# A two-block transformer kernel: end of a gate product, memory scores, squares and latent keys put in other places

## Chip, core and metric

The kernel runs as one program on one core of a Trainium2 chip. The metric is the device time of one execution in microseconds (us); less is better. TensorE (PE) multiplies, VectorE (DVE), ScalarE (ACT) and GpSimd (POOL) do elementwise work, SyncE (SP) issues most transfers. Each engine runs its own instructions strictly in order and waits on semaphores for the others.

## What is computed

Two transformer blocks over 512 rows of 1024 features, in float32. The first block mixes a short convolution, latent attention (MLA, 8 heads) and retention (4 heads) with 16 meta tokens ahead; the second sums three gated branches (gated linear attention, GLA; sparse attention, DSA; attention to a memory, MEM) and ends in 16 experts. What matters here:

```
y = concatenate([y_conv, y_mla, y_ret]);  x = x + y @ w_out        # first block
h = rmsnorm(x, g_mix)                                              # "h2" in the kernel
...
k = rmsnorm(mem_h @ w_kv keys);  o_mem = softmax(q k^T) v          # 4 heads of 256
gate = sigmoid(h @ w_gates + b)
merged = gate0*(o_gla @ w_o_gla) + gate1*(o_dsa @ w_o_dsa) + gate2*(o_mem @ w_o_mem)
x = x + merged @ w_out_2;  x = x + experts(rmsnorm(x))
```

## The kernel before

Every weight product is kept at nearly full float32 precision with three matmuls for one: weights and activations are split into a rounded part (`w_hi`, `act_hi`) and the rest (`w_lo`, `act_lo`). Weights arrive in units of 128 x 1024 into four slots of `raw`. For each unit ScalarE writes `w_hi` by a copy with rounding (`split_high`), then GpSimd subtracts it for `w_lo` (`split_low`). A product such as `gate10` is four units (u0 to u3), each met by four blocks of 128 rows (b0 to b3; memory products have b0 and b1). A `part` is one unit with one block: 2 chunks x 3 matmuls of 128 x 128 x 512, and one accumulating PSUM bank per block. `split_upto` places the split of the unit two ahead at the part with b0.

One list, `make_order()`, is walked by all engines; each has a function for a step or skips it. So the list sets the order of every engine. `spread(these, those)` puts the steps of `those` evenly between the steps of `these`: the parts of products fill TensorE's time while heads go through scores, softmax and values.

- MLA: `mla_transposes(h)` turns queries and keys of head h into `qT` and `kT` (h % 2 picks the buffer). ScalarE copied `qT` from PSUM bank 6 and VectorE copied `kT` (96 x 528) from banks 4 and 5 (`k_transposed`). Between the two heads of a pair stand parts of `ret_qk`; VectorE rotates each finished block of it (`rope_turn`, six operations).
- Norm of h2: `norm_scale("h2")` is four squares on ScalarE with row sums (`Square`, 128 x 1024), a reciprocal root in small steps shared by ScalarE (Ln, Exp) and VectorE, then four scalings on VectorE into `xs`. `norm("h2")` turns them on TensorE. `mem_scale("k")` is the same root for the memory keys `mk`, after `mem_kv0` and `mem_kv1`.
- DSA: 32 pairs j (8 heads x 4 blocks of rows). Step j has `dsa_scores(j)`, one or two parts, `dsa_values(j-2)` and `dsa_turn(j-1)`, which waits for the scaled probabilities of VectorE. `mix_dsa(h)` splits a head's output for the product `w_o10` into `mix_hi` (ScalarE) and `mix_lo` (VectorE). When all of `w_o01` is done, the waiting ones go out together.
- MEM: 16 pairs in the same pattern, with parts of `gate20` between.

When the last block of a gate product is accumulated, ScalarE loads the sigmoid table, waits for VectorE's four `gate_sum`, does a sigmoid of 128 x 2048 and loads the old table back.

Of the kernel before, what the change touches and what calls it, by code (L numbers as in the profile page):

```python
# [17 lines left out]
ACTF = mybir.ActivationFunctionType  # L18
# [227 lines left out]
def make_order():  # L246
# [4 lines left out]
    order += [("mla_norm", t) for t in range(2, NT + 1)] + item("mla_z")  # L251
    order += mla_order() + item("mem_kv0") + [("barrier", "gla"), ("norm_scale", "h2")] + item("mem_kv1") + [("mem_scale", "k")]
    order += item("mem_kv2") + [("norm", "h2"), ("mem_prepare", "k")] + item("mem_kv3")
# [59 lines left out]
def program(nc, w, out, known):  # L313
# [12 lines left out]
    with ExitStack() as ctx:  # L326
# [625 lines left out]
        def _(pe):  # L952
# [118 lines left out]

            def attention_transposes(tag, h, width, q_bank, k_bank, q_src, k_src):
# [6 lines left out]
                claim(k_bank, (DVE, ("kT", tag, h)))  # L1079
                claim(k_bank + 1, (DVE, ("kT", tag, h)))  # L1080
                pe.transpose(ps[0:width, k_bank, SEQ - N_META:SEQ], k_src(NT)[0:N_META, :], ident[0:N_META, 0:N_META])
                for t in range(NT):
                    tr = pe.transpose(ps[0:width, k_bank + 1, P * t:P * t + P], k_src(t), ident[:, :])
                tr.then_inc(*PE.done(("kT", tag, h)))

            def mla_scores(j):
                _, t, h, i = turn_of(j)
                n = P * (t + 1)
                if t == 0:
                    pe.wait_ge(*ACT.after("qT", "mla", h))  # L1090
                    pe.wait_ge(*DVE.after("kT", "mla", h))
# [38 lines left out]
            def mla_transposes(h):  # L1130
                if h == 0:
                    pe.wait_ge(*DVE.after("rope_m", "q", NT - 1, 5))
                    pe.wait_ge(*DVE.after("rope_m", "k", NT, 5))
                attention_transposes("mla", h, QKH, 6, 4, lambda t: q_sb[:, t, QKH * h:QKH * (h + 1)],
                                     lambda t: k_sb[:, t, QKH * h:QKH * (h + 1)])

            def ret_transposes(p):
                if p == 0:
                    pe.wait_ge(*DVE.after("rope_r", NT - 1, 5))
                    pe.wait_ge(*DVE.after("rope_r", NT, 5))  # L1140
                attention_transposes("ret", p, P, 0, 1, lambda t: rqk[:, t, P * p:P * (p + 1)],
                                     lambda t: rqk[:, t, 256 + P * p:256 + P * (p + 1)])

# [504 lines left out]
        def _(act):  # L1648
# [21 lines left out]
            def rsqrt_start(key, v):  # L1670
# [5 lines left out]
                nc.scalar.activation(v[1], v[1], ACTF.Exp, scale=-0.5).then_inc(*ACT.done(("y0", *key)))  # L1676

            def norm_scale(name):

# [3 lines left out]
                if name == "mem":  # L1683
# [5 lines left out]
                    act.wait_ge(mem_landed, 32)  # L1689
                act.wait_ge(*DVE.after("ss0", name))  # L1690
                for i, (src, scaled, rows) in enumerate(tiles):
                    for key in NORM_NEEDS(name, i):
                        act.wait_ge(*key[0].after(*key[1]))
                    nc.scalar.activation(scaled, src, ACTF.Square,
                                         accum_out=ss[0:rows, 0, i:i + 1]).then_inc(*ACT.done(("ss", name, i)))
                n = len(tiles)
# [416 lines left out]
            def q_transposed(tag, h, width, dst, bank):  # L2113
# [80 lines left out]
            for step, *a in order:  # L2194
# [18 lines left out]
                elif step == "norm_scale":  # L2213
                    norm_scale(*a)
                elif step == "conv":
                    for b in range(2):
# [17 lines left out]
        def _(dve):  # L2234
# [14 lines left out]
            def norm_scale(name):  # L2249

                tiles = NORM_TILES[name]
                n = len(tiles)
                if name != "h":
                    dve.memset(ss[:, 0:3, 0:n], 1.0).then_inc(*DVE.done(("ss0", name)))
# [610 lines left out]

            def k_transposed(tag, h, width, dst, bank):
                dve.wait_ge(*PE.after("kT", tag, h))
                if h >= 2:
                    dve.wait_ge(*PE.after(*last_scores(h - 2)))
                dve.tensor_copy(dst[0:width, h % 2, :],  # L2870
                                psf[0:width, (bank + 1) * SEQ - N_META:(bank + 2) * SEQ]).then_inc(*DVE.done(("kT", tag, h)))

            def mla_scores(j):
# [91 lines left out]
            for step, *a in order:  # L2965
                if step == "constants":
                    dve.memset(ss[:, 0:3, 0:NT + 1], 1.0).then_inc(*DVE.done(("ss0", "h")))
# [3 lines left out]
                elif step == "part":  # L2971
                    if a[0] in META_COLS and a[2] == "meta":
                        meta_add(*a[0:2])
                    elif a[1] == n_units(a[0]) - 1:
                        evict(a[0], a[2])
                elif step == "mla_transposes":
                    k_transposed("mla", a[0], QKH, kT, 4)
                elif step == "dsa_turn":
# [86 lines left out]
```

## Time and profile before

| | |
|---|---|
| three runs | 1498.11 us median (1496.21 to 1498.94) |
| profiled execution | 1493.74 us, its span on the core 1491.9 us |
| mean granted TensorE clock | 0.957 |
| TensorE busy | 1358.6 us, 91% of the span |
| VectorE, ScalarE, GpSimd busy | 600.3, 533.5, 417.3 us |

The span is what the views below cover; 1.84 us of the profiled time lie around it. In a row of the timeline the first number is the start in us from the span's start, the second the duration, then engine, line of the source, operation, what it writes and reads, the count, and in brackets the idle time before it with the work that ended it. Where rows are merged (x4) the second number is the whole stretch.

### The profile page before, as it was taken

How to read it: one execution, taken by the hardware profiler on the slowest of the kernel's cores; microseconds unless marked ns; L12 is line 12 of the kernel's file. 1: busy time of each engine (PE TensorE's matmuls, PEld its weight loads, DVE VectorE, ACT ScalarE, POOL GpSimd, SP SyncE). 2: the span in 40 equal slices, each digit the busy share in tenths (PEclk: the TensorE clock that was granted, in tenths of full speed). 3: DMA queues.
4: the chain of work that ended last, by engine and by line, in shares of the span. 5: the costliest groups of instructions: out<-in, count | busy, mean ns of one | idle time of the engine just before them, and what ended most of it. 6: DMA issues, size and time to landing. Idle time of an engine off the chain costs nothing.

```text
span 1491.9 us, 16432 instructions
## 1 busy us (share of the span) xinstructions
PE 1358.6 (91%) x6192; PEld 1003.2 (67%) x6192; DVE 600.3 (40%) x1340; ACT 533.5 (36%) x947; POOL 417.3 (28%) x202
## 2 busy tenths in 40 slices
PE   4999889888989999999998899899899997799996
PEld 3778666556767776675776787688787786444443
DVE  2086644444350114435897444214333315222125
ACT  4352322334463446444433545223534323101111
POOL 3155311001555341322433222344105331000002
PEclk9999898998999999999999999999999997799999
DMA  4132432303335130221322111243016524889925
GB/s 141 57 106 57 127 113 79 95 29 99 121 109 183 57 113 15 85 71 52 90 92 78 43 57 64 89 145 98 8 65 203 191 77 170 355 309 375 333 79 185
DMA packets 76440, 179.62 MB, mean 120 GB/s; under 512 B 11182, under 2 KB 22756, under 8 KB 69700
## 3 DMA queue, kind: packets, MB, share of 16 engines
q1 hardware_dynamic: 68656, 165.48, 33.0%
q0 software_dynamic: 2592, 8.41, 1.5%
q10 hardware_dynamic: 5108, 4.62, 1.1%
q8 instruction: 52, 0.85, 0.2%
q14 instruction: 32, 0.26, 0.1%
HBM read 153.32 MB, written 25.17 MB: 120 GB/s over the span
## 4 chain that ended last, share of the span: by engine, by line
PE 42%; DVE 9%; ACT 2%; issue 1%; DMA 1%; POOL 0%; DVEq 0%; ACTq 0%
PE ps L963 8%; PE ps L1445 8%; PE ps L965 7%; PE ps L964 7%; PE ps L1452 4%; DVE work L2512 1%; PE ps L1322 1%; DVE dq L2521 1%; DVE best L2510 1%; PE ps L1339 1%; PE ps L1438 1%; PE ps L1295 1%; PE ps L1367 1%; DVE mix_lo L2285 1%; PE ps L1329 1%
## 5 line engine op out<-in xcount | busy, mean ns | idle before, releaser
L847 POOL TENSOR_TENSOR w_lo<-raw,w_hi 128x1024 fp32r<-128x1024 f32 (+1 forms) x158 | 379.0, 2415 | 817.5 <-ACT w_hi L1659 817.5
L963 PE MATMUL ps<-w_hi,act_hi 128*128 128x512 f32 (+1 forms) x560 | 236.7, 423 | 6.5 <-POOL w_lo L847 3.6
L1659 ACT ACTIVATE w_hi<-raw 128x1024 fp32r<-128x1024 f32 (+1 forms) x158 | 158.7, 1032 | 182.2 <-PE ps L965 175.0
L964 PE MATMUL ps<-w_lo,act_hi 128*128 128x512 f32 (+1 forms) x560 | 221.6, 396 | 0.0
L965 PE MATMUL ps<-w_hi,act_lo 128*128 128x512 f32 (+1 forms) x560 | 220.8, 394 | 0.0
L963 PE MATMUL ps<-w_hi,mix_hi 128*128 128x512 f32 x320 | 132.8, 415 | 15.3 <-DVE mix_lo L2285 11.8
L963 PEld LDWEIGHTS ps<-w_hi,act_hi 128*128 128x128 f32 (+1 forms) x560 | 106.0, 189 | 46.6 <-issue 14.4
L965 PE MATMUL ps<-w_hi,mix_lo 128*128 128x512 f32 x320 | 128.0, 400 | 0.0
L964 PE MATMUL ps<-w_lo,mix_hi 128*128 128x512 f32 x320 | 127.9, 400 | 0.0
L965 PEld LDWEIGHTS ps<-w_hi,act_lo 128*128 128x128 f32 (+1 forms) x560 | 105.5, 188 | 25.6
L964 PEld LDWEIGHTS ps<-w_lo,act_hi 128*128 128x128 f32 (+1 forms) x560 | 105.9, 189 | 24.8 <-issue 2.5
L1445 PE MATMUL ps<-gu,xeT 128*128 128x512 f32 x256 | 117.5, 614 | 1.6 <-DVE xeT L2734 1.6
L963 PE MATMUL ps<-act_hi,w_hi 128*128 128x512 f32 (+4 forms) x280 | 105.5, 379 | 8.9 <-POOL w_lo L847 8.4
L964 PE MATMUL ps<-act_lo,w_hi 128*128 128x512 f32 (+4 forms) x280 | 105.6, 379 | 0.0
L965 PE MATMUL ps<-act_hi,w_lo 128*128 128x512 f32 (+4 forms) x280 | 104.4, 376 | 0.0
L1445 PEld LDWEIGHTS ps<-gu,xeT 128*128 128x128 f32 x256 | 49.2, 197 | 58.8 <-issue 58.8
L963 PEld LDWEIGHTS ps<-w_hi,mix_hi 128*128 128x128 f32 x320 | 62.1, 194 | 31.1 <-DVE mix_lo L2285 12.9
L964 PEld LDWEIGHTS ps<-w_lo,mix_hi 128*128 128x128 f32 x320 | 62.1, 194 | 13.6 <-issue 0.7
L965 PEld LDWEIGHTS ps<-w_hi,mix_lo 128*128 128x128 f32 x320 | 62.0, 194 | 13.5
L963 PEld LDWEIGHTS ps<-act_hi,w_hi 128*128 128x128 f32 (+2 forms) x280 | 52.3, 187 | 21.9 <-issue 5.6
L924 POOL DMA_INDIRECT yg<-y_rows,pos_main x8 | 8.4, 1054 | 194.2 <-DMA y_rows<-ye 192.1
L965 PEld LDWEIGHTS ps<-act_hi,w_lo 128*128 128x128 f32 (+2 forms) x280 | 52.5, 188 | 12.0 <-issue 1.3
(451 smaller groups left out, 1994.0 us busy)
## 6 DMA issues: line engine op xcount, KB each, us to landing
raw<-in_w_in SPq DMA_DIRECT2D x92, 512.0 KB, 3.6
gu<-in_w_gate SPq DMA_DIRECT2D x16, 1024.0 KB, 6.3
gu<-in_w_up SPq DMA_DIRECT2D x16, 1024.0 KB, 8.4
dn<-in_w_down SPq DMA_DIRECT2D x16, 1024.0 KB, 9.7
x_rows<-zeros SPq DMA_DIRECT2D x16, 512.0 KB, 4.9
raw<-in_w_out SPq DMA_DIRECT2D x16, 512.0 KB, 3.9
raw<-in_w_mem_kv SPq DMA_DIRECT2D x16, 512.0 KB, 3.6
xe<-x_rows SPq DMA_DIRECT2D x16, 512.0 KB, 9.1
```

What stands on the lines that cost most here:

```text
L847: pool.tensor_tensor(lo[:, 0:a], raw[:, g % RAW_SLOTS, 0:a], hi[:, 0:a].bitcast(F32), ALU.subtract).then_inc(*POOL.done(("w_lo", g)))
L963: pe.matmul(dst, l_hi, r_hi, start=start, stop=False, skip_group_check=skip)
L964: pe.matmul(dst, l_hi, r_lo, start=False, stop=False, skip_group_check=skip)
L965: return pe.matmul(dst, l_lo, r_hi, start=False, stop=stop, skip_group_check=skip)
L1295: pe.matmul(ps[:, bank, 0:n], iqT[rows, h // 2, P * t:P * t + P], ikT[rows, 0:n], start=True, stop=True).then_inc(*PE.done(("rel", t, h)))
L1322: pe.matmul(ps[:, 4 + j % 2, 0:n], dqT[:, h, P * t:P * t + P], dkT[:, h // DSA_G, 0:n], start=True, stop=True).then_inc(*PE.done(("d_S", j)))
L1329: tr = pe.transpose(ps[:, 6, P * b:P * b + P], d_prob[:, j % 3, P * b:P * b + P], ident[:, :])
L1339: mm = pe.matmul(ps[:, 7, P * t:P * t + P], dv[:, b, P * g:P * g + P], d_probT[:, j % 2, P * b:P * b + P], start=(b == 0), stop=(b == t))
L1367: mm = pe.matmul(ps[:, 4 + j % 2, 0:MEM], mqT[:, 2 * h + c, P * t:P * t + P], mkT[:, 2 * h + c, :], start=(c == 0), stop=(c == 1))
L1445: mm = pe.matmul(ps[:, bank, :], xeT[:, i, k, :], gu[s][:, :, k, :], start=(k == 0), stop=(k == KC - 1))
L1452: mm = pe.matmul(ps[:, 5 + n, :], hidT[:, i, P * c:P * c + P], dn[s][:, c, 512 * n:512 * n + 512], start=(c == 0), stop=(c == 1))
L1659: nc.scalar.activation(split_slot(g)[0][:, 0:a], raw[:, g % RAW_SLOTS, 0:a], ACTF.Copy).then_inc(*ACT.done(("w_hi", g)))
```

## The change

Four places of the order, and one move between engines:

1. Of the 48 parts of `gate01`, `w_o01` and `gate10` between the sparse pairs, the last four (`gate10` u3, b0 to b3) now stand behind the last `mix_dsa`, just ahead of `w_o10`. The other 44 are spread over the 35 steps, so 9 steps have two parts where 13 had.
2. At the first memory scores a part of `gate20` stands after pair 0 and one after pair 1; one stood there after pair 1 alone.
3. The four squares of the norm of h2 stand between the parts of `mem_kv1`, one ahead of each pair of parts; what follows of `norm_scale` stands behind `mem_kv1`.
4. The copies of the latent keys `kT` go from VectorE to ScalarE, behind those of `qT`.

```diff
-    order += mla_order() + item("mem_kv0") + [("barrier", "gla"), ("norm_scale", "h2")] + item("mem_kv1") + [("mem_scale", "k")]
+    order += mla_order() + item("mem_kv0") + [("barrier", "gla"), ("norm_square", "h2", 0)]
+    order += [x for i in range(1, NT) for x in item("mem_kv1")[2 * i - 2:2 * i] + [("norm_square", "h2", i)]]
+    order += item("mem_kv1")[6:] + [("norm_scale", "h2"), ("mem_scale", "k")]
...
-    for step in [x for s in spread(steps, [[p] for p in item("gate01", "w_o01", "gate10")]) for x in s]:
+    dense = item("gate01", "w_o01", "gate10")
+    for step in [x for s in spread(steps, [[p] for p in dense[:-4]]) for x in s]:
...
-    order += done + item("w_o10", "gate11", "w_o11", "mem_q0") + [("mem_scale", "q0")]
+    order += done + dense[-4:] + item("w_o10", "gate11", "w_o11", "mem_q0") + [("mem_scale", "q0")]
...
-    order += [x for s in spread(steps, [[p] for p in g2 if p[3] < 3]) for x in s] + [p for p in g2 if p[3] == 3]
+    free = [p for p in g2 if p[3] < 3]
+    order += steps[0] + free[0:1] + steps[1] + free[1:2]
+    order += [x for s in spread(steps[2:], [[p] for p in free[2:]]) for x in s] + [p for p in g2 if p[3] == 3]
...
+            def norm_square(name, i):
+
+                if i == 0:
+                    act.wait_ge(*DVE.after("ss0", name))
+                src, scaled, rows = NORM_TILES[name][i]
...
+                nc.scalar.activation(scaled, src, ACTF.Square,
+                                     accum_out=ss[0:rows, 0, i:i + 1]).then_inc(*ACT.done(("ss", name, i)))
...
+            def k_transposed(tag, h, width, dst, bank):
+                act.wait_ge(*PE.after("kT", tag, h))
+                nc.scalar.activation(dst[0:width, h % 2, :], psf[0:width, (bank + 1) * SEQ - N_META:(bank + 2) * SEQ],
+                                     ACTF.Copy).then_inc(*ACT.done(("kT", tag, h)))
...
                 elif step == "mla_transposes":
                     q_transposed("mla", a[0], QKH, qT, 6)
+                    k_transposed("mla", a[0], QKH, kT, 4)
```

ScalarE from the end of `mem_kv0` (`xs` is a square's output, `w_hi` a unit's split, `ss` 128x4 the root for h2 and 128x8 that for the memory keys, `m_sq` and `mk` the squares and copy of a finished memory block, `mv_new` a block of `mem_kv2`). Before:

```order
L1694 ACTIVATE xs,ss<-x_56 128x1024 x4
L1674 ACTIVATE ss<-ss 128x4
L1676 ACTIVATE ss<-ss 128x4
L1659 ACTIVATE w_hi<-raw 128x1024 x4
L1838 ACTIVATE m_sq<-ps 128x512
L1840 ACTIVATE mk<-ps 128x512
L1838 ACTIVATE m_sq<-ps 128x512
L1840 ACTIVATE mk<-ps 128x512
L1674 ACTIVATE ss<-ss 128x8
L1676 ACTIVATE ss<-ss 128x8
L1659 ACTIVATE w_hi<-raw 128x1024 x4
L1840 ACTIVATE mv_new<-ps 128x512 x2
```

Now, from the third split of this stretch; three squares with two splits between them stand ahead of it:

```order
L1664 ACTIVATE w_hi<-raw 128x1024
L1690 ACTIVATE xs,ss<-x_56 128x1024
L1664 ACTIVATE w_hi<-raw 128x1024
L1850 ACTIVATE m_sq<-ps 128x512
L1852 ACTIVATE mk<-ps 128x512
L1850 ACTIVATE m_sq<-ps 128x512
L1852 ACTIVATE mk<-ps 128x512
L1679 ACTIVATE ss<-ss 128x4
L1681 ACTIVATE ss<-ss 128x4
L1679 ACTIVATE ss<-ss 128x8
L1681 ACTIVATE ss<-ss 128x8
L1664 ACTIVATE w_hi<-raw 128x1024 x4
```

The four splits that stood behind all squares now stand one behind each square, and both roots have moved together, right ahead of the next four splits.

VectorE at the same place, from the last step of the root for h2 (`xs` are the four scalings, the reduction of `m_sq` a memory block's sum). Before:

```order
L2246 SCALAR_TENSOR_TENSOR ss<-ss 128x4
L2260 TENSOR_SCALAR xs<-x_56,ss 128x1024 x4
L2392 TENSOR_REDUCE ss<-m_sq 128x2 x2
L2237 TENSOR_SCALAR ss<-ss 128x8
L2242 SCALAR_TENSOR_TENSOR ss<-ss 128x8
L2244 TENSOR_TENSOR ss<-ss 128x8
L2246 SCALAR_TENSOR_TENSOR ss<-ss 128x8
L2521 TENSOR_TENSOR mk<-mk,ss 128x1024 x2
```

Now:

```order
L2266 SCALAR_TENSOR_TENSOR ss<-ss 128x4
L2280 TENSOR_SCALAR xs<-x_56,ss 128x1024 x4
L2257 TENSOR_SCALAR ss<-ss 128x8
L2262 SCALAR_TENSOR_TENSOR ss<-ss 128x8
L2264 TENSOR_TENSOR ss<-ss 128x8
L2266 SCALAR_TENSOR_TENSOR ss<-ss 128x8
L2541 TENSOR_TENSOR mk<-mk,ss 128x1024 x2
```

The memory sums no longer stand behind the scalings, but the memory root (128x8) still does, now with nothing of TensorE's in between.

ScalarE at the end of the sparse heads (`d_probT` copies turned probabilities, `dqT` takes the output of the last head, `mix_hi` is its rounded part, `gate` the sigmoid of `gate10`). Before:

```order
L2031 ACTIVATE d_probT<-ps 128x384
L1659 ACTIVATE w_hi<-raw 128x1024
L2031 ACTIVATE d_probT<-ps 128x512
L2037 ACTIVATE dqT<-ps 128x512
L1667 ACT_TABLE_LOAD
L1808 ACTIVATE gate<-gate 128x2048
L1667 ACT_TABLE_LOAD
L2042 ACTIVATE mix_hi<-dqT 128x512
L1659 ACTIVATE w_hi<-raw 128x1024 x4
L2202 DMA gate_bias<-in_b_gate 128x512
```

Now:

```order
L1664 ACTIVATE w_hi<-raw 128x1024
L2043 ACTIVATE d_probT<-ps 128x512
L2049 ACTIVATE dqT<-ps 128x512
L2054 ACTIVATE mix_hi<-dqT 128x512
L1664 ACTIVATE w_hi<-raw 128x1024
L1672 ACT_TABLE_LOAD
L1820 ACTIVATE gate<-gate 128x2048
L1672 ACT_TABLE_LOAD
L1664 ACTIVATE w_hi<-raw 128x1024 x4
L2219 DMA gate_bias<-in_b_gate 128x512
```

`mix_hi` of the last head now stands right behind `dqT`, ahead of the sigmoid and its two table loads, and the split of a `w_o10` unit has moved behind it.

## Rows read from the trace of the kernel before

**Rows 1.** The page: busy time of TensorE, and GpSimd's group of low parts.

```profile
PE 1358.6 (91%) x6192; PEld 1003.2 (67%) x6192; DVE 600.3 (40%) x1340; ACT 533.5 (36%) x947; POOL 417.3 (28%) x202
...
L847 POOL TENSOR_TENSOR w_lo<-raw,w_hi 128x1024 fp32r<-128x1024 f32 (+1 forms) x158 | 379.0, 2415 | 817.5 <-ACT w_hi L1659 817.5
```

**Rows 2.** Stretches of TensorE: length, busy time (count), granted clock, DMA share, GB/s.

```profile
221.30:233.50 12.20, 10.76 (x35) 0.50 0.01 2
416.60:421.20 4.60, 4.57 (x11) 0.50 0.49 155
855.60:858.40 2.80, 2.75 (x12) 0.50 0.00 0
939.10:943.80 4.70, 4.62 (x11) 0.50 0.18 38
943.80:948.80 5.00, 5.00 (x24) 0.99 0.55 177
1060.50:1063.50 3.00, 2.93 (x11) 0.53 0.37 90
...
407.10:437.20 30.10, 25.42 (x97) 0.89 0.36 115
```

**Rows 3.** Timeline, TensorE and VectorE, at the scores of latent head 2.

```profile
220.41 0.70 DVE L2870 COPY kT<-ps 96x528 f32<-96x528 f32 x1
...
221.26 0.58 PE L1097 MATMUL ps<-kT,qT 96*128 96x16 f32 x2 [2.78 <-DVE kT L2870]
...
225.04 0.42 DVE L2300 TENSOR_TENSOR t<-ps,rope 128x256 f32<-128x256 f32 x1 [2.06 <-PE ps L965]
...
227.72 0.37 PE L1106 MATMUL ps<-ident,prob 128*16 128x128 f32 x1 [1.44 <-DVE rqk L2405]
```

**Rows 4.** Timeline at the norm of h2, with the same scaling at the start.

```profile
16.97 2.74 DVE L2260 TENSOR_SCALAR xs<-x,ss 128x1024 f32<-128x1024 f32 x4
...
408.99 1.04 ACT L1694 ACTIVATE xs<-x 128x1024 f32<-128x1024 f32 x1
...
412.89 3.88 ACT L1659 ACTIVATE w_hi<-raw 128x1024 fp32r<-128x1024 f32 x4
...
413.60 9.09 DVE L2260 TENSOR_SCALAR xs<-x,ss 128x1024 f32<-128x1024 f32 x4
...
416.63 0.79 PE L963 MATMUL ps<-w_hi,mem_hi 128*128 128x512 f32 x1 [3.80 <-POOL w_lo L847]
```

**Rows 5.** Timeline, ScalarE and TensorE, at the end of the sparse heads.

```profile
931.03 0.60 ACT L2037 ACTIVATE dqT<-ps 128x512 f32<-128x512 f32 x1 [1.69 <-PE ps L1339]
...
934.55 1.91 ACT L1808 ACTIVATE gate<-gate 128x2048 f32<-128x2048 f32 x1 [1.62 <-DVE gate L2362]
...
937.77 0.63 ACT L2042 ACTIVATE mix_hi<-dqT 128x512 fp32r<-128x512 f32 x1
...
939.18 0.79 PE L963 MATMUL ps<-w_hi,mix_hi 128*128 128x512 f32 x1 [5.39 <-DVE mix_lo L2285]
```

**Rows 6.** Timeline, TensorE's waits between the sparse pairs, and VectorE's five splits.

```profile
825.86 0.66 PE L1329 MATMUL ps<-ident,d_prob 128*128 128x128 f32 x4 [1.08 <-DVE d_prob L2565]
...
855.65 1.65 PE L1339 MATMUL ps<-d_probT,dv 128*128 128x128 f32 x6 [3.10 <-ACT d_probT L2031]
...
895.28 3.10 DVE L2285 SCALAR_TENSOR_TENSOR mix_lo<-dqT,mix_hi 128x512 fp32r<-128x512 f32 x5 [1.12 <-ACT mix_hi L2042]
...
899.24 0.66 PE L1329 MATMUL ps<-ident,d_prob 128*128 128x128 f32 x4 [1.36 <-DVE d_prob L2565]
...
928.06 0.66 PE L1329 MATMUL ps<-ident,d_prob 128*128 128x128 f32 x4 [0.82 <-DVE d_prob L2565]
```

**Rows 7.** Timeline, VectorE and TensorE, between the memory pairs.

```profile
1056.31 2.50 DVE L2521 TENSOR_TENSOR mq<-mq,ss 128x512 f32<-128x512 f32 x4
...
1060.57 0.69 PE L1376 MATMUL ps<-ident,m_prob 128*128 128x128 f32 x2 [2.93 <-DVE m_prob L2565]
...
1089.88 1.22 PE L1387 MATMUL ps<-m_probT,mv 128*128 128x128 f32 x8 [0.42 <-ACT m_probT L2072]
```

More of the change, by code:

```diff
@@ L1070, in norm, with attention_transposes @@
                     tr.then_inc(*PE.done(("T", name, "meta")))
-            def attention_transposes(tag, h, width, q_bank, k_bank, q_src, k_src):
+            def attention_transposes(tag, h, width, q_bank, k_bank, q_src, k_src, k_copier):
                 claim(q_bank, (ACT, ("qT", tag, h)))
@@ L1078, in attention_transposes @@
                 tr.then_inc(*PE.done(("qT", tag, h)))
-                claim(k_bank, (DVE, ("kT", tag, h)))
-                claim(k_bank + 1, (DVE, ("kT", tag, h)))
+                claim(k_bank, (k_copier, ("kT", tag, h)))
+                claim(k_bank + 1, (k_copier, ("kT", tag, h)))
                 pe.transpose(ps[0:width, k_bank, SEQ - N_META:SEQ], k_src(NT)[0:N_META, :], ident[0:N_META, 0:N_META])
@@ L1090, in mla_scores @@
                     pe.wait_ge(*ACT.after("qT", "mla", h))
-                    pe.wait_ge(*DVE.after("kT", "mla", h))
+                    pe.wait_ge(*ACT.after("kT", "mla", h))
                 at = score_at(t)
@@ L1134, in mla_transposes @@
                 attention_transposes("mla", h, QKH, 6, 4, lambda t: q_sb[:, t, QKH * h:QKH * (h + 1)],
-                                     lambda t: k_sb[:, t, QKH * h:QKH * (h + 1)])
+                                     lambda t: k_sb[:, t, QKH * h:QKH * (h + 1)], ACT)
             def ret_transposes(p):
@@ L1141, in ret_transposes @@
                 attention_transposes("ret", p, P, 0, 1, lambda t: rqk[:, t, P * p:P * (p + 1)],
-                                     lambda t: rqk[:, t, 256 + P * p:256 + P * (p + 1)])
+                                     lambda t: rqk[:, t, 256 + P * p:256 + P * (p + 1)], DVE)
             def ret_scores(p, part):
@@ L1676, in rsqrt_start @@
                 nc.scalar.activation(v[1], v[1], ACTF.Exp, scale=-0.5).then_inc(*ACT.done(("y0", *key)))
+            def norm_square(name, i):
+                if i == 0:
+                    act.wait_ge(*DVE.after("ss0", name))
+                src, scaled, rows = NORM_TILES[name][i]
+                for key in NORM_NEEDS(name, i):
+                    act.wait_ge(*key[0].after(*key[1]))
+                nc.scalar.activation(scaled, src, ACTF.Square,
+                                     accum_out=ss[0:rows, 0, i:i + 1]).then_inc(*ACT.done(("ss", name, i)))
             def norm_scale(name):
@@ L1689, in norm_scale @@
                     act.wait_ge(mem_landed, 32)
[L1690 to L1695, printed above, removed]
+                if ("norm_square", name, 0) not in order:
+                    for i in range(len(tiles)):
+                        norm_square(name, i)
                 n = len(tiles)
@@ L2214, in _ @@
                     norm_scale(*a)
+                elif step == "norm_square":
+                    norm_square(*a)
                 elif step == "conv":
@@ L2252, in norm_scale @@
                 n = len(tiles)
-                if name != "h":
+                if name != "h" and ("norm_square", name, 0) not in order:
                     dve.memset(ss[:, 0:3, 0:n], 1.0).then_inc(*DVE.done(("ss0", name)))
@@ L2864, in mla_norm @@
                     rope_turn(("rope_m", kind, t), x3[:, :, QKN:QKH], x3[:, :, QKN:QKH], rows, MLA_H, QKR // 2, t, cos_m, sin_m)
[L2866 to L2871, printed above, removed]
             def mla_scores(j):
@@ L2965, in _ @@
             for step, *a in order:
-                if step == "constants":
+                if step == "norm_square" and a[1] == 0:
+                    dve.memset(ss[:, 0:3, 0:len(NORM_TILES[a[0]])], 1.0).then_inc(*DVE.done(("ss0", a[0])))
+                elif step == "constants":
                     dve.memset(ss[:, 0:3, 0:NT + 1], 1.0).then_inc(*DVE.done(("ss0", "h")))
@@ L2975, in _ @@
                         evict(a[0], a[2])
-                elif step == "mla_transposes":
-                    k_transposed("mla", a[0], QKH, kT, 4)
                 elif step == "dsa_turn":
```

## The prediction

> **What bounds the kernel now.** I read the page first, then the trace as a timeline, then the granted clock by stretches. The page says that TensorE is busy 1358.6 of the span's 1491.9 us, no other engine over 41% [rows 1]. So a change of order is worth what it takes out of TensorE's waits, and of the time in which TensorE runs at a low clock. The second counts as much as the first. In four stretches of 2.8 to 12.2 us the granted clock is 0.50, that is 1.2 of 2.4 GHz, and each begins right behind a wait of TensorE: 2.78 us [rows 3] ahead of 221.3, 3.80 [rows 4] ahead of 416.6, 3.10 [rows 6] ahead of 855.6, 5.39 [rows 5] ahead of 939.1. A fifth, at 0.53, follows 2.93 us [rows 7] at 1060.5. In 939.1 to 943.8 there are 11 matmuls in 4.7 us (0.43 us each); in the 5 us behind, at 0.99, 24 starts are counted (0.21; I use 0.23, since the counts at the edges blur) [rows 2]. So 11 matmuls at the low clock cost 11 x 0.20 = 2.2 us beside the wait. The waits of 1.08, 1.36, 0.82 and 0.42 us [rows 6, 7] need not be so followed.
>
> All four edits lie at such a wait. What stands behind them on TensorE is dense product work, which starts sooner if TensorE arrives sooner; SyncE's weight loads, ScalarE's and GpSimd's splits follow TensorE's progress through the four slots (GpSimd waited 817.5 us for ScalarE's splits [rows 1]), so time gained at one place is not paid back at the next.
>
> **Edit 1, the end of gate10.** Before, the last head's output was copied by ScalarE at 931.03 to 931.63, but its rounded part waited until 937.77, behind a table load and the sigmoid, which itself waited for VectorE's last sum (934.55), and a second load. TensorE had no work for 5.39 us, then 11 slow matmuls [rows 5, 2]. Now `mix_hi` stands right behind that copy: it ends some 1.3 us after the last values, `mix_lo` 0.62 later (3.10 for five [rows 6]), while TensorE has six parts, 36 matmuls x 0.23 = 8.3 us. The sigmoid now ends some 1.6 us plus its 1.91 after TensorE's last gate part, the table 1.3 later; the third unit of `w_o10`, split behind it (0.97 + 2.4), is there at about 7.2, needed at 8 parts x 1.4 = 11.2. So both the wait and the slow stretch go: -5.39 - 2.2 = -7.6 us. The four bank claims of `w_o10` wait for sums that VectorE makes one part behind TensorE: nothing.
>
> What it costs inside the loop. Four of the thirteen steps with two parts have one. A part only fills; where the chain scores, maximum, exponential, scaling is shorter than one part and the values, nothing is lost, and most steps with one part show no wait. One place gets worse. All of `w_o01` ends in step 25 instead of 23, so the first flush of `mix_dsa` has six heads instead of five, and the step behind it has one part instead of two. Before, five `mix_lo` held VectorE for 3.10 us and TensorE waited 1.36 [rows 6]. Now six hold it 3.7, and 1.4 us of filling is missing: measured from the turn that releases the flush, the scaled probabilities come at about +6.1 us and TensorE is done at +2.3, a wait of 3.8, or +2.4 more. Behind a wait of that length a slow stretch follows: the one behind 3.10 us lasted 2.8 us [rows 2], half of which is lost, +1.4. The wait of 0.82 at 928.06 [rows 6] came from a gate sum ahead of the scaling in VectorE's order; it moves behind the loop, -0.8. Waits of the kind at 825.86 (1.08, a scaling that meets GpSimd's w_lo) come where a split falls in a step ahead of one with a single part; by the new list some two go and two or three come: 0, up to +1.5. Edit 1: -7.6 + 2.4 + 1.4 - 0.8 = **-4.6**; bounds -7.6 (no new wait) and -2.5.
>
> **Edit 2, the first memory scores.** TensorE waited 2.93 us at 1060.57 for the first scaled probabilities [rows 7]. VectorE was scaling `mq` until 1058.81 and only then took the maximum of pair 0 [rows 7], so scores 1, made one part later, are still in time: costs nothing. The part between fills 6 x 0.23 = 1.4 us of the wait; 1.5 stay. I take it that the clock then stays up, since 1.36 at 899.24 was followed by a normal pace and 2.93 was not: 3.0 us at 0.53 lose 1.4 [rows 2]. One more step is without a part; such a step showed 0.42 [rows 7]. -1.4 - 1.4 + 0.4 = **-2.4**; bounds -2.8 and 0.
>
> **Edit 3, the squares.** Before, the four squares (1.04 each and a read of the sum) and the root stood ahead of four splits (3.88), and TensorE waited 3.80 for GpSimd [rows 4]. From 407.1 to 437.2 there are 96 matmuls, 22.7 us at full pace, in 30.1 [rows 2]: 7.4 us of waits and low clock. Now splits and squares alternate, 1.2 + 1.0 us a pair, GpSimd keeps 2.4 us a unit [rows 1], and the units of `mem_kv1` come at about 412.6 and 415.0, needed at 412.8 and 415.6. Those waits go. But the root for the memory keys stands right behind that of h2, ScalarE's part of it waits for VectorE's mean, and on VectorE the four scalings stand ahead of that mean. What is queued behind it on ScalarE are the last two splits of `mem_kv2`, and GpSimd and TensorE wait for those. The last square sum of `mem_kv1` ends at about 419.9, the root at 421.1, the scalings 2.7 later (2.74 for four and a small one's start, GpSimd idle [rows 4]), ScalarE's Ln and Exp at 424.5, split 425.7, GpSimd 428.4. TensorE has used up its work at 407.1 + 72 x 0.2365 = 424.1: a new wait of 4.3 us, with 2.2 behind it for the clock. 6.5 instead of 7.4: **-0.9**. Bounds: -7.4 if the new wait is absent, +2 if GpSimd comes later.
>
> Here a rule could change the sum. The four scalings took 2.74 us at the start and 9.09 in 413.60 to 422.69, when GpSimd made low parts, 2.27 each [rows 4]. The Trainium skill, page "SBUF — State Buffer", section "Who interferes with whom", says that VectorE in a two-port mode and GpSimd take one port pair in turn, each fully blocked while the other holds it; the trace agrees (2.27 against 0.68). By the trace alone, as by this rule, the scalings are fast only if GpSimd is idle at 421, which it is by my walk (its last unit ends at 419.8).
>
> **Edit 4, the latent keys.** At head 2 VectorE had six rotations ahead of the copy `kT` (220.41 to 221.11); TensorE, idle since 218.48, waited 2.78 us and then ran slow until 233.5 [rows 3, 2]. ScalarE was free: its copy of the keys would end at about 219.15 (0.6 for 96 columns of 512 and more, against 0.70), so scores start at 219.25, 2.0 earlier. But the next wait stays. TensorE's next turn needs bank 4, freed by VectorE behind the rotation of the last block, 225.04 to 227.72, 2.7 us after that block is done [rows 3]. Now the block is done at 221.5 and the turn starts at 224.2, TensorE being out of work at 222.1: a wait of 2.1 where it was 1.44, 3.5 us earlier in time. From there the old run took 5.8 us at 0.50 to 233.5, worth 2.9 at full clock. With no slow stretch the gain is 3.5 + 2.9 = 6.4; with one of 2.8 to 4.6 us [rows 2] behind the 2.1 us wait, 4.1 to 5.0. I take **-4.5**, as the wait is nearer to 2.78 than to 1.36; bounds -6.5 and -1. At the other heads VectorE was free and the copy waits for TensorE: nothing.
>
> **Sum.** -4.6 - 2.4 - 0.9 - 4.5 = -12.4 us. On the profiled execution, 1493.74, that gives 1481.3. That one lies 4.4 under the median of the runs; on the median, 1498.11, it gives **1485.7**.
>
> **The rivals**, on the median.
> - *All four waits go.* The new wait of edit 3 does not arise, for instance since the splits of `mem_kv2` are two units ahead. For it: TensorE needs the third only at 424.1. Against it: the list of ScalarE. -7.4 instead of -0.9: 1479.2.
> - *Loop and clock give half back.* More of the single-part steps wait, the clock stays low behind 1.5 us at the memory scores and as long as before at head 2: edit 1 -2.5, edit 2 -1, edit 4 -1: with -0.9, 1492.7. For it: 12.2 us at 0.50 behind two waits.
> - *The scalings meet GpSimd again.* 9.1 instead of 2.7 us, the new wait 6.4 longer: 1492.1. It decides if GpSimd's unit starts before 421; my margin is 1.4 us.
> - *The edits do nothing.* Waits only change places: what the end gains the loop loses, 4.3 + 2.2 stands for 7.4, and head 2 waits for VectorE anyway: 1497 to 1499. Against it: the 5.39 us were ScalarE's order alone.
> - *Slower.* The sparse loop falls to the low clock and stays there. Each part then costs 6 x 0.20 = 1.2 us more. Ten slow parts beyond the stretch I count use up the gain; fourteen give 12.4 x 14/10 - 12.4 = +4.9, 1503. For it: nothing but the long stretch at 221.3; before, the loop recovered in 2.8 us behind its longest wait [rows 2].
>
> **How the numbers follow.** Chances: forecast 0.60, all waits go 0.10, half given back 0.12, scalings 0.06, nothing 0.07, slower 0.05. The likeliest case has its own range of 1482 to 1490. The range reaches down to all waits gone and up to half given back: 1478 to 1493, about 0.8 of the cases. A difference under 0.2% (3 us) is no change for this kernel's measurement. Faster: 0.60 + 0.10 + 0.12 + 0.06 = 0.88; same 0.07; slower 0.05.
>
> **What the profile after would show.** Step by step: no wait of TensorE ahead of `w_o10`, and clock 1.0 there; a wait over 3 us for `d_prob` behind the six `mix_hi`; about 1.5 us ahead of the first memory turn at full clock; no wait for `w_lo` within `mem_kv1` and one near 4 us at the third unit of `mem_kv2`, with ScalarE's Ln of the memory root behind VectorE's scalings; scores of head 2 released by ScalarE within 1 us, and 2 us of wait at the next turn. The forecast is wrong if the low-clock stretches stay as long though the waits go, or if the loop shows waits in many single-part steps.

## The result, and the profile after

| | before | changed |
|---|---|---|
| runs, median (range) | 1497.8 us (1496.21 to 1498.94) | 1477.69 us (1469.1 to 1482.56) |
| profiled execution, its span | 1493.74, 1491.9 us | 1482.56, 1480.7 us |
| mean granted TensorE clock in it | 0.957 | 0.961 |

The ratio is 0.9866, with a 95% interval of 0.9845 to 0.9886: 20.1 us faster where I had forecast 12.4, and 0.3 us under the low end of my range. The four runs lie at 1469.1, 1474.66, 1480.72 and 1482.56 us, at mean clocks of 0.971, 0.965, 0.960 and 0.961. The profiled one is the longest of them, 4.9 us over their median, and the profiled one of before lies 4.1 under its median, so the rows show only 11.2 of the 20.1 us.

The page of the changed kernel answers to [rows 1]:

```profile
PE 1353.6 (91%) x6192; PEld 999.6 (68%) x6192; DVE 586.5 (40%) x1332; ACT 537.8 (36%) x955; POOL 416.7 (28%) x202
```

TensorE is still the bound. The timeline of the changed kernel at latent head 2 answers to [rows 3]; each row is start, duration, engine and what it does, with the wait before it in brackets:

```profile
219.82 0.61 ACT L2133 ACTIVATE kT<-ps 96x528 f32<-96x528 f32 x1
...
220.58 0.37 PE L1102 MATMUL ps<-kT,qT 96*128 96x16 f32 x2 [0.79 <-ACT kT L2133]
...
225.35 0.27 PE L1111 MATMUL ps<-ident,prob 128*16 128x128 f32 x1 [2.02 <-DVE rqk L2425]
```

ScalarE now copies the keys in 0.61 us, the scores wait 0.79 instead of 2.78, and the next turn 2.02 instead of 1.44. At the norm of h2, against [rows 4]:

```profile
422.78 2.74 DVE L2280 TENSOR_SCALAR xs<-x,ss 128x1024 f32<-128x1024 f32 x4
...
425.64 0.21 ACT L1679 ACTIVATE ss<-ss 128x8 f32<-128x8 f32 x1 [3.48 <-DVE ss L2257]
...
430.21 0.67 PE L968 MATMUL ps<-w_hi,mem_hi 128*128 128x512 f32 x1 [4.31 <-POOL w_lo L852]
```

The scalings take 2.74 us where they took 9.09, but ScalarE's `Ln` of the memory root waits 3.48 us for VectorE, and TensorE waits 4.31 at the third unit of `mem_kv2`. At the sparse pairs and the first memory turn, against [rows 5 to 7]:

```profile
812.67 0.33 PE L1334 MATMUL ps<-ident,d_prob 128*128 128x128 f32 x1 [1.87 <-DVE d_prob L2585]
...
816.04 0.44 PE L1334 MATMUL ps<-ident,d_prob 128*128 128x128 f32 x2 [0.78 <-DVE d_prob L2585]
...
852.24 1.16 PE L1344 MATMUL ps<-d_probT,dv 128*128 128x128 f32 x8 [1.94 <-ACT d_probT L2043]
...
893.45 3.70 DVE L2305 SCALAR_TENSOR_TENSOR mix_lo<-dqT,mix_hi 128x512 fp32r<-128x512 f32 x6 [1.51 <-ACT mix_hi L2054]
...
898.15 0.69 PE L1334 MATMUL ps<-ident,d_prob 128*128 128x128 f32 x2 [3.69 <-DVE d_prob L2585]
...
913.95 0.44 PE L1334 MATMUL ps<-ident,d_prob 128*128 128x128 f32 x2 [1.60 <-DVE d_prob L2585]
...
924.32 0.63 ACT L2054 ACTIVATE mix_hi<-dqT 128x512 fp32r<-128x512 f32 x1
...
931.77 0.39 PE L968 MATMUL ps<-w_hi,mix_hi 128*128 128x512 f32 x1
...
1050.85 0.44 PE L1381 MATMUL ps<-ident,m_prob 128*128 128x128 f32 x2 [1.52 <-DVE m_prob L2585]
```

`w_o10` starts at 931.77 with no bracket: there is no wait ahead of it. The six `mix_lo` hold VectorE for 3.70 us, and the turn behind them waits 3.69. The first memory turn waits 1.52 instead of 2.93. So every wait of the forecast is there, each within 0.2 us of it. The sum was wrong all the same.

The second half of the cost is the granted clock. Here are stretches of TensorE in the kernel before, not shown above (columns as in [rows 2]), and then in the changed kernel:

```profile
295.00:305.00 10.00, 7.98 (x56) 1.00 0.01 2
...
813.00:818.00 5.00, 4.30 (x12) 0.66 0.20 61
```

```profile
222.00:232.00 10.00, 7.98 (x49) 0.83 0.01 2
295.00:305.00 10.00, 9.31 (x44) 0.50 0.00 0
305.00:312.00 7.00, 6.21 (x35) 0.82 0.00 0
...
812.00:817.00 5.00, 3.55 (x16) 1.00 0.26 59
...
898.00:903.00 5.00, 4.85 (x14) 0.66 0.15 52
1050.00:1055.00 5.00, 3.51 (x23) 1.00 0.19 52
```

I reckon the loss of a stretch as its length x (1 - clock). At head 2 the 12.2 us at 0.50 lost 6.1; now 1.7 us are lost (10 x 0.17). Two things I had not looked for stand beside that. At 295 to 312 the changed kernel runs at 1.2 of 2.4 GHz for more than 10 us and loses 6.3 us so reckoned (5.0 + 1.3), though no wait there is over 1.3 us; the kernel before was at full clock. Behind the wait of 1.87 us at the first sparse turns, the same in both kernels, the kernel before lost 1.7 us (0.66) and the changed one nothing. And behind the new wait of 3.69 us 1.7 us are lost, as forecast (1.4).

### The profile page after: what moved, and what is told of

Read it like the earlier page. It is cut to its first block, busy times and chain, and to the rows that moved or that the text cites. A ratio compares the mean times of both kernels' runs of the same rounds, so it can differ in the third digit from the quotient of the medians.

```text
span 1480.7 us, 16426 instructions
## 1 busy us (share of the span) xinstructions
PE 1353.6 (91%) x6192; PEld 999.6 (68%) x6192; DVE 586.5 (40%) x1332; ACT 537.8 (36%) x955; POOL 416.7 (28%) x202
## 4 chain that ended last, share of the span: by engine, by line
PE 42%; DVE 8%; ACT 2%; issue 1%; DMA 1%; POOL 0%; DVEq 0%; ACTq 0%
PE ps L968 8%; PE ps L1450 8%; PE ps L969 8%; PE ps L970 8%; PE ps L1457 4%; DVE work L2532 1%; PE ps L1344 1%; PE ps L1327 1%; DVE dq L2541 1%; DVE best L2530 1%; PE ps L1443 1%; PE ps L1300 1%; DVE mix_lo L2305 1%; PE ps L1372 1%; PE ps L1334 1%
```

## The experiments

Each is compared with the kernel before on the same chip, in three groups (e1 to e4, e5 to e8, e9 to e12); the medians of before were 1495.78, 1495.2 and 1495.89 us, over 28, 18 and 17 runs.

| run | median us (runs) | ratio to before, 95% interval |
|---|---|---|
| e1 gate end alone | 1485.62 (7) | 0.9931 [0.9906, 0.9955] |
| e2 keys alone | 1485.84 (10) | 0.994 [0.9921, 0.9959] |
| e3 squares alone | 1495.7 (12) | 1.0 [0.9984, 1.0016] |
| e4 memory scores alone | 1492.84 (12) | 0.9983 [0.9968, 0.9998] |
| e5 all four, again | 1474.35 (6) | 0.9873 [0.9845, 0.9901] |
| e6 two gate parts behind the last mix | 1487.09 (7) | 0.9949 [0.9929, 0.9968] |
| e7 all four, memory root later | 1474.2 (4) | 0.9858 [0.9831, 0.9884] |
| e8 before, with two squares more at the start | 1497.36 (12) | 1.0011 [0.9994, 1.0027] |
| e9 thin loop alone | 1496.92 (12) | 1.0004 [0.9993, 1.0016] |
| e10 all four, one head's mix a turn | 1478.41 (5) | 0.9878 [0.9858, 0.9897] |
| e11 e7 and e10 together | 1472.82 (5) | 0.9848 [0.9828, 0.9867] |
| e12 e6, edits 2 to 4, memory root later | 1473.17 (6) | 0.9862 [0.9839, 0.9885] |

### The four edits one by one

The diff of each is its own lines of the change, on the kernel before. First the end of `gate10` (edit 1):

> Only edit 1 (the last four parts of gate10 behind the last mix_dsa). Theory A, waits decide and each low-clock stretch hangs on the wait ahead of it: the wait of 5.39 us ahead of w_o10 and its slow stretch go, a wait near 3.7 us appears behind six mix_hi; -4.6 us in the profile and in the median. Theory B, the granted clock elsewhere is redrawn whenever the work moves in time: the waits are the same as in A, but the total differs from -4.6 by several us either way, and the difference lies in stretches at low clock behind waits that the edit did not touch.

Measured: -10.3 us in the median (interval -14.1 to -6.7), well beyond my -4.6. Outside the sparse loop and the memory pairs TensorE's order is the same in all these kernels, and each trace has all 6192 matmuls, so the n-th matmul of one can be set beside the n-th of another. From the matmul that starts at 801.2 us in the kernel before to the one at 947.4, around the sparse loop and its end, e1's profile takes 9.8 us less. So what I missed lies in the stage that the edit touches, and not, as theory B has it, behind other waits.

The latent keys (edit 4):

> Only edit 4 (latent keys copied by ScalarE). Theory A: -4.5 us (head 2's scores 2 us sooner, less low clock up to 233 us), nothing at the other heads. Theory B: the same waits, but a total between -10 and +3 us, by low-clock stretches elsewhere; in the changed kernel's profile the gain of 4.9 us at head 2 was followed by a new slow stretch near 295 to 310 us that took 5.6 us back.

Measured: -9.0 us (-11.8 to -6.1), twice my -4.5. The timeline of this run shows both waits as in the changed kernel:

```profile
218.19 0.37 PE L1097 MATMUL ps<-kT,qT 96*128 96x16 f32 x2 [0.79 <-ACT kT L2128]
...
223.00 0.27 PE L1106 MATMUL ps<-ident,prob 128*16 128x128 f32 x1 [2.02 <-DVE rqk L2420]
```

and its stretch of TensorE behind them has the full clock:

```profile
225.00:235.00 10.00, 10.00 (x66) 1.00 0.35 107
```

The same wait of 2.02 us was followed by 0.83 in the changed kernel's profile (above). From the matmul at 216.2 us of before to the one at 243.6 this profile gains 6.4 us, which is my full-clock case.

The squares (edit 3):

> Only edit 3 (squares between the parts of mem_kv1). Both theories: no wait for w_lo inside mem_kv1, one of 4.3 us at the third unit of mem_kv2. Theory A: -0.9 us in all, no difference that can be measured. Theory B: more than 3 us either way, through low-clock stretches elsewhere.

Measured: no difference in the median (-2.4 to +2.4). The new wait is there, 4.32 us for 3.80:

```profile
429.63 0.50 PE L965 MATMUL ps<-w_hi,mem_hi 128*128 128x512 f32 x1 [4.32 <-POOL w_lo L849]
```

From the matmul at 395.4 us of before to the one at 459.8 this profile takes 1.6 us less, which the median can't show.

The memory scores (edit 2):

> Only edit 2 (parts behind memory pairs 0 and 1). Theory A: -2.4 us, the wait ahead of the first turn 1.5 us at full clock. It stands late in the program, so nothing ahead of it moves: theory B also gives -2.4 up to that place, and then differs only in the stretches at low clock behind it (the routing waits from 1180 us on).

Measured: -2.5 us (-4.8 to -0.3), as forecast, and the wait is the forecast one:

```profile
1059.54 0.44 PE L1378 MATMUL ps<-ident,m_prob 128*128 128x128 f32 x2 [1.54 <-DVE m_prob L2576]
```

That the number fits so well is partly chance: from 1049.9 to 1111.2 us of before this profile, and each of the six others with edit 2, gains 1.5 us. The four medians add up to -21.8, near the -20.1 of all together. Their intervals together leave some 6 us either way; within that no loss or gain from their meeting shows. The large differences from the forecast sit in edit 1 and edit 4.

### The changed kernel again, and the kernel before shifted in time

e5 is the changed kernel without any edit.

> The changed kernel once more, for a second profile and more runs. Theory A (each low-clock stretch is fixed by the wait ahead of it): the slow stretch near 295 to 310 us, which took back 5.6 us, stands there again, and so does 1236 at the routing. Theory B (it is drawn anew in each execution, whatever the order): it can be absent, the total then nearer 1475 than 1482; the runs spread over some 10 us.

Measured: 1474.35 us; its six runs lie at 1469.58, 1470.18, 1471.88, 1476.82, 1479.5 and 1480.04, at clocks of 0.971, 0.970, 0.968, 0.963, 0.962 and 0.961. The profiled one has a span of 1467.7 us against 1480.7, with the same order and the same waits in the loop:

```profile
842.38 1.16 PE L1344 MATMUL ps<-d_probT,dv 128*128 128x128 f32 x8 [1.93 <-ACT d_probT L2043]
...
888.26 0.69 PE L1334 MATMUL ps<-ident,d_prob 128*128 128x128 f32 x2 [3.69 <-DVE d_prob L2585]
...
904.08 0.44 PE L1334 MATMUL ps<-ident,d_prob 128*128 128x128 f32 x2 [1.61 <-DVE d_prob L2585]
```

Its stretches at the places that were slow before:

```profile
222.00:232.00 10.00, 9.11 (x61) 1.00 0.16 48
295.00:305.00 10.00, 8.90 (x54) 1.00 0.00 0
305.00:312.00 7.00, 7.00 (x58) 1.00 0.01 4
```

All three are at full clock. Taking 10 us windows over the first 1460 us, behind which TensorE has next to no work, and adding up 10 x (1 - clock), 54.7 us are lost to the low clock in the first profile and 39.2 in this one: 15.5 us, against 13.0 us between the spans. The sum counts idle time at the low clock too, so it is too large. The starts of the same matmuls show the price. Here is the last wait ahead of the slow stretch of the first profile and one behind it, then the same two in e5:

```profile
293.16 0.40 PE L1102 MATMUL ps<-kT,qT 96*128 96x16 f32 x2 [1.27 <-DVE probT_m L2912]
...
309.18 0.36 PE L1102 MATMUL ps<-kT,qT 96*128 96x16 f32 x2 [0.79 <-ACT kT L2133]
```

```profile
289.12 0.40 PE L1102 MATMUL ps<-kT,qT 96*128 96x16 f32 x2 [1.28 <-DVE probT_m L2912]
...
299.30 0.37 PE L1102 MATMUL ps<-kT,qT 96*128 96x16 f32 x2 [0.79 <-ACT kT L2133]
```

The first profile is 4.0 us late at the upper row and 9.9 at the lower. It falls behind by 2.5 us at 171 to 184, 1.5 at 225 to 230, 5.8 here, 1.6 near 1181 and 1.6 at 1225 to 1240. That is all of the 13.0, and at each of these places it has more low clock than e5. So this is theory B: in one order with the same waits the clock falls in one execution and not in the other.

e8 asks whether the clock turns on where in time the work falls. Two squares more stand ahead of the first norm:

```diff
+                if name == "h":
+                    for t in range(2):
+                        nc.scalar.activation(xs[:, t, :], x1[:, t, :], ACTF.Square).then_inc(*ACT.done(("shift", t)))
+                    act.wait_ge(*ACT.after("shift", 1))
```

> The kernel before with two more squares of 128 x 1024 on ScalarE ahead of the first norm (their outputs are written over), so that all the rest comes 2.1 us later with the same waits. Theory A: +2.1 us, 1497.9. Theory B (the low clock depends on when in time a wait falls, not on its length alone): between -4 and +8, with low-clock stretches appearing or going at waits of the same length.

Measured: +1.6 us by the ratio (-0.9 to +4.0), close to the 2.1 added. A shift of all work by 2 us gains or loses no more than 3 us beside itself. Its profile is at low clock from 223.2 to 233.4 and 298.3 to 305.1 us, and e1 and e9, which are not shifted, have the same two stretches some 1.3 us earlier.

### What the thinner loop costs

e6 leaves the loop as thick as before and puts only its last two parts behind the last `mix_dsa`:

```diff
-    order += done + item("w_o10", "gate11", "w_o11", "mem_q0") + [("mem_scale", "q0")]
+    order = order[:-2] + done + order[-2:] + item("w_o10", "gate11", "w_o11", "mem_q0") + [("mem_scale", "q0")]
```

> The kernel before, with only the last two gate10 parts behind the last mix_dsa; the loop keeps all else and no step loses a part. If thinning the loop costs what I forecast (+3.8 us for the six-head flush and its low clock), this one is faster than edit 1 alone: the 5.39 us wait and its slow stretch gone, the 0.82 wait kept, -7.6 us, or more than edit 1 alone by the cost of the loop. If the thinner loop costs nothing, as e1 suggests (-10.2), it is no better than e1: -7.6 to -9.5.

Measured: -7.6 us (-10.6 to -4.6), which fits my price for the end (5.39 + 2.2); the loop is as before. e1, which has the thinner loop, should then stand 3 us behind it by my sum; it stands 2.7 ahead (within the intervals).

e9 does the reverse. It spreads only 44 parts and puts the last four ahead of the last mix:

```diff
+    dense = item("gate01", "w_o01", "gate10")
+    for step in [x for s in spread(steps, [[p] for p in dense[:-4]]) for x in s]:
...
+    order += dense[-4:] + done + item("w_o10", "gate11", "w_o11", "mem_q0") + [("mem_scale", "q0")]
```

> The kernel before with the 44 parts of edit 1 spread over the sparse pairs, but the last four parts of gate10 standing together behind the loop and AHEAD of the last head's mix. So the loop is as thin as in the change, and the order of ScalarE at its end (sigmoid ahead of the rounded part of the last head, no product work of TensorE in between) is as before. Theory A (my term in the prediction): the thinner loop costs 3.0 us (2.4 of longer wait, 1.4 of low clock, 0.8 back) and the 5.39 us wait ahead of w_o10 stays: about +3, ratio 1.002. Theory B (what the profile of the change and the run with only two parts behind suggest): the single-part steps' waits go for what the six-head mix costs, so the loop costs nothing: 0 (-1 to +1), ratio 1.000. Theory C: the thinner loop is a gain of its own, -3 or more, ratio 0.998 or less; then much of edit 1's 10 us does not come from the end at all.

Measured: 1.0004 [0.9993, 1.0016], or +0.6 us (-1.0 to +2.4). Theory A's +3 is outside, and so is theory C's gain; theory B holds. Its timeline has the same new wait as the changed kernel, and the old one ahead of `w_o10`:

```profile
818.90 0.44 PE L1330 MATMUL ps<-ident,d_prob 128*128 128x128 f32 x2 [0.51 <-DVE d_prob L2575]
...
855.10 1.16 PE L1340 MATMUL ps<-d_probT,dv 128*128 128x128 f32 x8 [1.93 <-ACT d_probT L2039]
...
859.15 0.44 PE L1330 MATMUL ps<-ident,d_prob 128*128 128x128 f32 x2 [0.54 <-DVE d_prob L2575]
...
900.16 0.44 PE L1330 MATMUL ps<-ident,d_prob 128*128 128x128 f32 x2 [3.69 <-DVE d_prob L2575]
...
916.01 0.44 PE L1330 MATMUL ps<-ident,d_prob 128*128 128x128 f32 x2 [1.60 <-DVE d_prob L2575]
...
939.39 0.79 PE L964 MATMUL ps<-w_hi,mix_hi 128*128 128x512 f32 x1 [5.39 <-DVE mix_lo L2295]
```

and behind the last one the clock is low for the whole 5 us:

```profile
938.00:940.00 2.00, 0.61 (x2) 0.67 0.00 0
940.00:945.00 5.00, 5.00 (x13) 0.50 0.36 102
```

So in this profile the end's order costs 5.39 + 2.5 and some 0.3 for the first matmuls, 8.2 us, against 7.6 in my sum. The profiles agree: from the first sparse scores to the first memory turn e9's takes 1.2 us less than before and e1's 9.8 less, a difference of 8.6.

e10 takes the 3.69 us wait away, on the changed kernel:

```diff
-            order, done = order + done, []
+            order, done = order + done[:1], done[1:]
```

> The changed kernel with the rows of finished heads split for w_o10 one head behind each turn, not six at once. It takes the wait of 3.69 us behind the six away (VectorE then has 0.6 us of splits ahead of a turn instead of 3.1). If that wait is paid in full: -2.3 (down to the 1.36 of a single step) to -3.7 against the changed kernel; with the low clock that I forecast behind it 1.4 more, so -5. If a later wait takes its place, as VectorE's splits of the other heads stand in the single-part steps that follow: 0 to -1. The split of each head now stands in five later steps, 0.6 us each, so each of those may wait 0.6 longer.

Measured: 0.9878 [0.9858, 0.9897], no better than the changed kernel. The wait is gone from its place and stands at others:

```profile
895.13 0.44 PE L1334 MATMUL ps<-ident,d_prob 128*128 128x128 f32 x2 [0.68 <-DVE d_prob L2585]
...
900.84 0.55 PE L1334 MATMUL ps<-ident,d_prob 128*128 128x128 f32 x3 [1.18 <-DVE d_prob L2585]
...
912.66 0.44 PE L1334 MATMUL ps<-ident,d_prob 128*128 128x128 f32 x2 [2.73 <-DVE d_prob L2585]
```

Two more waits there are 0.36 us each. These are the waits of the kernel before that [rows 6] does not show:

```profile
813.70 0.33 PE L1329 MATMUL ps<-ident,d_prob 128*128 128x128 f32 x1 [1.87 <-DVE d_prob L2565]
...
836.59 0.55 PE L1329 MATMUL ps<-ident,d_prob 128*128 128x128 f32 x3 [0.66 <-DVE d_prob L2565]
...
902.90 0.33 PE L1329 MATMUL ps<-ident,d_prob 128*128 128x128 f32 x1 [0.29 <-DVE d_prob L2565]
...
920.32 0.44 PE L1329 MATMUL ps<-ident,d_prob 128*128 128x128 f32 x2 [0.72 <-DVE d_prob L2565]
```

Added up over the loop without the end, TensorE waits 9.9 us before, 10.1 in e9, 9.9 in the changed kernel (the five rows of the first section) and 9.9 in e10. All of these waits but one in each kernel end on VectorE's `d_prob`, and an edit of the loop moves them. That the four sums agree so closely may be chance; no run here shows why they should.

### The memory root later

e7 is the changed kernel with `mem_scale("k")` four parts into `mem_kv2`:

```diff
-    order += item("mem_kv1")[6:] + [("norm_scale", "h2"), ("mem_scale", "k")]
-    order += item("mem_kv2") + [("norm", "h2"), ("mem_prepare", "k")] + item("mem_kv3")
+    order += item("mem_kv1")[6:] + [("norm_scale", "h2")] + item("mem_kv2")[0:4] + [("mem_scale", "k")]
+    order += item("mem_kv2")[4:] + [("norm", "h2"), ("mem_prepare", "k")] + item("mem_kv3")
```

> The changed kernel with the memory root (mem_scale of k) four parts later, behind the splits of mem_kv2's third and fourth unit. My account of edit 3: the wait of 4.3 us at the third unit of mem_kv2 and the 1.7 to 2.2 us of low clock behind it go, so -6 us against the changed kernel: near 1471. Rival, the wait there comes from GpSimd's or the transfers' own pace: it only shrinks below 1 us' worth or moves a unit on, 1476 to 1478.

Measured: 1474.2 us, beside the 1474.35 of e5 and not the 1471 of my forecast. The 4.31 us wait is gone, and two other costs have come:

```profile
421.93 7.03 DVE L2280 TENSOR_SCALAR xs<-x,ss 128x1024 f32<-128x1024 f32 x4
...
429.07 0.21 ACT L1679 ACTIVATE ss<-ss 128x8 f32<-128x8 f32 x1 [5.87 <-DVE ss L2257]
...
435.40 3.29 PE L1067 MATMUL ps<-ident,xs 128*128 128x128 f32 x16 [2.83 <-DVE act_lo L2291]
```

With two splits ahead of them the scalings meet GpSimd again: 7.03 us, where they took 2.74 with GpSimd idle. (This is the rule of the Trainium skill, page "SBUF — State Buffer", section "Who interferes with whom", that the two engines hold one port pair in turn; the trace agrees, with 7.03 us for the four scalings against 2.74.) And TensorE waits 2.83 us at the turns of h2. From 395.4 to 459.8 us of before this profile gains 4.7 us, as do those of e11 and e12 below, and the changed one 1.6. So the later root is worth 3.1 us at its stage where I had forecast 6; four and six runs that spread over 7 and 10 us can't show it in the median.

### Both, and a candidate

> The changed kernel with one head's split a turn (as the run beside it) and the memory root four parts later (as the run before that measured 3.1 us better at its stage and equal in the median). If the gains add: -4 to -6 against the changed kernel, 1469; if what a profile shows at a stage is drowned in the clock of each execution: within 3 us of the changed kernel.

> The kernel before with edits 2, 3 and 4, the memory root four parts later, and of edit 1 only that the last two parts of gate10 stand behind the last mix (the loop is as thick as before). By the single runs: -2.5 (edit 2), 0 to -3 (edit 3 with the later root), -9 (edit 4), -7.6 (two parts behind): -19 to -22 against the kernel before, 1473 to 1476, as the changed kernel. If the thinner loop is a gain of its own (2 us or more) this one is that much slower than the changed kernel; if my forecast of its cost (+3.0) was right, 3 us faster.

Measured: 1472.82 and 1473.17 us, for e11 the second of its two cases, for e12 the sum of the single runs. Both intervals, 0.9828 to 0.9867 and 0.9839 to 0.9885, overlap that of the changed kernel. e12 has the thick loop and e11 the thin one, and their medians are alike: they show no cost of 3 us for the thin loop either. I can't call either better than the changed kernel.

## Why the prediction was wrong

Right were the direction, the bound, the mechanism of each edit and the waits: none ahead of `w_o10`; 3.69 us (3.8) behind the six `mix_hi`; 4.31 (4.3) at `mem_kv2`; 1.52 (1.5) at the memory turn; 0.79 and 2.02 (under 1, and 2) at head 2. Edit 2 was -2.4 and measured -2.5 in the median (-1.5 at its stage), edit 3 -0.9 and 0 (-1.6 at its stage). The time fell near that of "all four waits go" (1479.2), but not by it: the wait at `mem_kv2` is there. "Half given back" and "slower" are ruled out by the medians, and "the scalings meet GpSimd" did not happen in the changed kernel but did in e7.

**The first step that failed is "What it costs inside the loop".** I added +2.4 for the longer wait and +1.4 for the clock behind it, and counted the other waits of the loop as "some two go and two or three come: 0". The wait and its low clock came. But 1.08 [rows 6] went, and 0.66, 0.29 and 0.72 that I had not shown; 0.78 and 1.60 came; and the wait of 3.10 fell to 1.94. The loop's waits are 9.9 us in both kernels, and in these two profiles the low clock behind them (813 to 818 before, 898 to 903 now) only changed its place. With 0.82 taken off I had the loop at +3.0; e9 measured +0.6 (-1.0 to +2.4). I had worked out one new wait in full and put the rest at nothing, though several stood in the trace. The removed end was slightly under-priced too, 7.6 against 8.2 to 8.6; in e9's profile the clock was low for longer than the 11 matmuls that I counted. One sum in that step was off without harm: the third unit of `w_o10` comes at 1.6 + 1.91 + 1.3 + 0.97 + 2.4 = 8.2 us and not 7.2, still ahead of 11.2, and the changed kernel has no wait there.

**The second is the clock term of edit 4.** I took -4.5, "as the wait is nearer to 2.78 than to 1.36", so that low clock would follow it. Seven profiles have the old order at head 2 (before, e1, e3, e4, e6, e8, e9) and seven the new (changed, e2, e5, e7, e10, e11, e12). Reckoned as above, the old ones lose 6.8, 5.1, 1.7, 6.8, 5.2, 5.1 and 5.2 us to the clock from 210 to 240, mean 5.1; the new ones 1.7, 0, 0, 1.7, 1.7, 0 and 0, mean 0.7. By the starts of the same matmuls, four of the new profiles gain 6.4 or 6.5 us at head 2 on the profile that I read, which is my "no slow stretch" case (-6.4), and three gain 4.9, near my case of a short stretch (-5.0): the mean is -5.8, so the term was 1.3 us too small. But the profile that I read was itself a slow one there, by 1.1 us against the mean of the seven. Kind against kind the edit is worth 4.6 us at head 2, so that my -4.5 fits that stage by luck: it took too much low clock in the new order and too much in the old. The -9.0 of e2 is not explained by it; 1.3 us more lie at 244 to 395 us, and the rest I can't place.

Here are all fourteen profiles by stage, each as its difference from the profile before (whose own 0 is in the means of the first column):

| stage, in us of the kernel before | order of before | with the edit |
|---|---|---|
| 216.2 to 243.6 | six at -2.9 to 0.0, mean of the seven -1.1 | edit 4: three at -4.9, four at -6.4 or -6.5, mean -5.8 |
| 243.6 to 395.4 | six at 0.0 to +5.8, mean of the seven +2.8 | edit 4: seven at -0.5 to +5.4, mean +1.5 |
| 395.4 to 459.8 | six at -0.8 to +0.2, mean of the seven -0.3 | edit 3: four at -1.5 or -1.6; with the later root three at -4.7 |
| 801.2 to 947.4 | four at -1.3 to +0.8, mean of the five -0.5; e9 -1.2 | edit 1: six at -8.3 to -9.8, mean -8.9; e6 -7.9, e12 -6.1 |
| 1049.9 to 1111.2 | six at -0.6 to +1.0, mean of the seven 0.0 | edit 2: seven at -1.5 |

Kind against kind, edit 1 is worth 8.4 us where I had 4.6. That is about half of the 7.7 us between forecast and result, and the thin loop, if anything, is a gain: e9 lies 0.7 us under the mean of its kind, and the six with the whole edit lie under e6 and e12. Edit 2 is worth 1.5 (forecast 2.4), edit 3 1.3 (0.9), edit 4 4.6 at its head (4.5) and, with wide spread, 1.3 behind it (nothing). These add up to -17.1, the upper end of the interval of the result (-23.2 to -17.1); about 3 us of the 20.1 stay unplaced.

**Not a term but a limit** is what one profile can tell. The changed kernel's ten runs fall from 1469.1 to 1482.56 us, and the time goes with the clock: those of 1470.18 and less have 0.970 or 0.971, those of 1479.5 and more 0.960 to 0.962. Six of the ten are under my low end. My sum of -12.4 lies close to the first profile's -11.2, but only because that one has the stretch at 295 to 312 beside the gains that I missed. In the seven profiles of the old order the loss from 280 to 320 is 0, 3.4, 5.2, 0, 3.4, 3.4 and 3.4 us, in the seven of the new 6.9, 0, 0, 6.9, 1.7, 0 and 0. The two go together: the four new profiles with full clock at head 2 lose nothing at 280 to 320 either, and the three that lose 1.7 at head 2 are those that lose there. The profile before showed none there, so no row could have given me either the loss or its absence. My range took the bounds of each term, but nothing for the clock at places that the change does not touch.

Left open: what decides, in one order with the same waits, whether the clock falls. The shift by 2 us (e8) did not show it, and no run tests anything else.

## What to carry to other kernels

When an edit thins the filler of a loop, list all its waits before and after, not only the new one: here they summed to 9.9 us either way, and a wait taken out by hand came back at the next head. A small step that the bounding engine needs, queued behind a table load and a large activation, is worth its whole wait and the low clock behind it: over 8 of the 20 us. Where the clock falls behind waits of 2 to 3 us in some executions only, price that term by several profiles of both kernels, or carry it as a range of its own. And where two kernels give an engine the same order, set the n-th instruction of one trace beside the n-th of the other: here that showed 1.5 us at a stage in seven profiles alike, where medians of 12 runs leave more than 2 us open.

## What was not expected of the hardware

The same instructions with the same waits ran at different clocks. After the wait of 2.02 us at head 2 the granted clock was 0.83 over the next 10 us in one execution and 1.00 in another; at 295 to 305 it was 0.50 and 1.00, with waits of no more than 1.3 us in both. The six runs of one kernel on one chip lie 10 us apart with it, 1469.58 to 1480.04 (mean clock 0.971 and 0.961), 0.7% of the time.
